# A decoder layer with routed experts: one expert instead of two loaded ahead of the route, and eight narrow tiles instead of seven

## The chip, the cores and the metric

One core of a Trainium2 chip runs the whole program. The metric is device time in microseconds (us) of one execution, lower is better; three executions of a kernel give its median. The engines are TensorE (PE in the rows), VectorE (DVE), ScalarE (ACT), GpSimd (POOL) and SyncE (SP). SP does nothing but ask for transfers; POOL asks for the gathers.

## The reference

One layer serves 512 prompt tokens and 64 sample tokens (576 in all, width 1024, all float32). After the mixing sub-layer (attention beside a spatial gate, then an output projection) comes a mixture of experts:

```python
h2 = rms_norm(x, g_pre_ffn) * (1 + sc2) + sh2
# hier_moe(h2): best of 4 groups, then top 2 of its 4 experts; 16 experts, weights from two softmaxes
for e in range(N_EXPERTS):
    hdn = jax.nn.silu(x @ w_gate[e]) * (x @ w_up[e])     # (N, 1024) @ (1024, 512), twice
    y = y + gates[:, e:e + 1] * (hdn @ w_down[e])        # (N, 512) @ (512, 1024)
x = x + ga2 * rms_norm(y, g_post_ffn)
```

Each token goes to two experts, so 1152 places are filled. `w_gate`, `w_up` and `w_down` of one expert are 2 MB each, 6 MB together, 96 MB for the sixteen.

## The kernel before

The program is one block after another: `condition`, `project`, `attend_prompt`, `attend_sample`, `merge`, `experts`, `later_tiles`, `combine`. Every engine has its own list of instructions, in the order of the code, and waits on semaphores.

**Tiles.** The tokens of an expert are gathered into a tile. `experts` handles MAIN = 16 tiles, one for each expert. A wide tile has 128 places, a narrow one 64 (`wide`, `places`, HALF). In a wide tile gate (line 2454) and up (line 2464) are two runs of eight 128x512 matmuls, and down (line 2489) is two more runs of four. In a narrow tile gate (line 2461) goes to one half of the output rows and up (line 2464) to the other, in turn, and down (line 2494) does the same with its two column halves. A matmul in float32 shows as two passes, so a run of eight has x16 in the trace. Lines 2426 and 2519 are the transposes of the gathered tokens and of h.

TensorE's order in tile e is: gate and up of e, the token transposes of e+1, down of e-1, the transposes of h of e. TILE_AT gives the number of the tile that is done at place e of the order; before it is 0, 1, 2, 4, 3, 6, 5, ..., 14, 13, 15. Tiles 0, 1, 2 and the even ones are wide (nine), the other seven narrow. The two tiles of the end (LAST) are narrow.

**Which expert is in which tile.** Experts 0 to FIXED-1 are always in tiles 0 to FIXED-1, whatever their number of tokens. The others are ranked by it at run time (`key`, `narrow`, `place` in VectorE's part of `merge`), the WIDE = 7 largest go to the wide tiles, the rest to the narrow ones. Tokens that do not fit go to overflow tiles of `later_tiles`, a loop that runs only if there are any.

**Loads.** Weights lie in a ring of eight slots of 2 MB; `expert_slot` gives slot and count for each (e, kind), kind being 0 for gate, 1 for up, 2 for down. Load q = 3e + kind needs the slot of load q-8, so SP waits for the end of gate, up or down of an earlier tile first. Those of fixed experts need no knowledge of the route. The loads of expert 0 are asked for at the end of `merge`, as soon as the sample group's attention has left its slots; so is gate of expert 1, behind them. Then come the five stores of h2 to memory (`store(t)`, line 1862), which the gathers read. Up and down of expert 1 are asked for once gather 0 has landed. Then SP waits for `order_done`, the semaphore that says which expert is in which tile, and from there on asks for tile after tile, with the store of the results of tile e-3 behind the loads of tile e.

**The h2 buffers.** The five tiles of h2 use two buffers in part: before h2 of tiles 2 and 3 is computed, VectorE waits until the store of tile 0 or 1 has landed:

```python
                if t in (2, 3):
                    dve.wait_ge(h2_out2[t % 2], 16)
```

Behind h2 of the last tiles come, on VectorE, the logits, the choice of experts and the ranks (`route`, `first`), all of it serial. Gather 0 needs `first_ready` and the stores of h2. VectorE makes the table of the other tiles after the first gate has been multiplied (`table`, line 2436), and then `order_done` (line 2093).

Of the kernel before, what the change touches and what calls it, by code (L numbers as in the profile page):

```python
# [23 lines left out]
P = 128  # L24
# [11 lines left out]
NE, DE = 16, 512  # L36
# [3 lines left out]
BIG = 1e37  # L40
UNIT = 4096
MAIN = NE
FIXED = 2
WIDE = 7
HALF = P // 2
OVER = 10
NTILE = MAIN + OVER
TILE_AT = [0, 1, 2] + [e + 1 if e % 2 else e - 1 for e in range(3, MAIN - 1)] + [MAIN - 1]
LAST = (MAIN - 3, MAIN - 1)
EARLY = 3  # L50
ZERO_ROW = 3 * P + HALF
# [8 lines left out]
def wide(e):  # L60


    return e < FIXED or e % 2 == 0


def rows(t):
# [4 lines left out]
def constant_table():  # L71

    p = np.arange(P)[:, None]
    cols = {}
    cols["ident"] = np.eye(P)
    x = np.arange(512)[None, :] - 384
    cols["dist"] = np.where(p - x >= 0, p - x, BIG)
    t, h = p % ST, p // 16
    slope = 2.0 ** -(h + 1.0)
    r = np.arange(120)[None, :] - 56  # L80
    cols["own"] = np.where((r >= 0) & (r <= t), -slope * (t - r), -BIG)
    cols["tril"] = (np.arange(P)[None, :] <= p) * 1.0
    c64 = np.arange(NS)[None, :]
    cols["sameseq"] = (c64 // ST == p // ST) * 1.0
    cols["repeat"] = (c64 % ST == p) * 1.0
    cols["before"] = (p < np.arange(P)[None, :]) * 1.0
    cols["ones"] = np.ones((P, P))
    e = np.arange(NE)
    cols["earlier"] = np.broadcast_to((e[None, :] < e[:, None]).reshape(1, -1), (P, NE * NE)) * 1.0
    cols["desc"] = np.broadcast_to([4.0, 3.0, 2.0, 1.0], (P, 4))  # L90
    cols["group"] = (p // 32 == np.arange(4)[None, :]) * 1.0
    cols["diag"] = ((p // ST) % 4 == np.arange(4)[None, :]) * 1.0
    row = (p // 16) * ST + t
    first = (p // ST) % 2 == 0
    cols["sel1"] = ((row == c64) & first) * 1.0
    cols["sel2"] = ((row == c64) & ~first) * 1.0
    cols["half"] = np.full((P, H), -0.5)
    cols["token"] = p + P * np.arange(NT)[None, :] * 1.0
    cols["row"] = np.broadcast_to(np.arange(P)[None, :] * 1.0, (P, P))
    cols["tilestart"] = np.broadcast_to(P * np.arange(NTILE + 1)[None, :] * 1.0, (P, NTILE + 1))  # L100
    cols["pagerow"] = p % PAGEROWS * 1.0
    tie = np.where(e < FIXED, 20000.0 - 1000.0 * e, NE - 1.0 - e)
    cols["tie"] = np.broadcast_to(tie[None, :], (P, NE))
    cols["place0"] = np.broadcast_to(np.where(e < FIXED, -128.0 * e, -256.0)[None, :], (P, NE))
    at, parts = {}, []
    n = 0
    for name, a in cols.items():
        a = np.broadcast_to(a, (P, a.shape[1]))
        at[name] = (n, a.shape[1])
        n += a.shape[1]  # L110
        parts.append(a)
    at["mainbase"] = at["tilestart"][0], NE
    at["index"] = at["row"][0], OVER

    past = -slope * (PAST + t - np.arange(PAST).reshape(2, P, ROWKEYS).transpose(0, 2, 1).reshape(1, PAST))
    return at, np.ascontiguousarray(np.concatenate(parts, 1).astype(np.float32)), \
        np.ascontiguousarray(past.astype(np.float32))
# [101 lines left out]
class Program:  # L219
# [614 lines left out]
    def attend_prompt(self, block):  # L834
# [3 lines left out]
        nc, a, o, L, PS = self.nc, self.a, self.o, self.L, self.PS  # L838
# [3 lines left out]
        dchain, pchain, zeroed = self.dve_chain, self.pool_chain, self.sem("c_zeroed")  # L842
# [38 lines left out]
        @block.gpsimd  # L881
        def _(pool):
            link = chain(pool, pchain, self.pool_count)

            pool.wait_ge(self.lam_sum, 1)
            pool.wait_ge(grp_done, 3 * NT)
            self.load_pages(pool, self.ck, 0, 0, K_SLOT[0][0])
            pool.wait_ge(self.ada_done, 3)
            self.load_pages(pool, self.ck, 0, 1, K_SLOT[0][1])
            self.load_pages(pool, self.cv, 0, 0, V_SLOT[0])  # L890

            link(pool.memset(L.mix[:, 4, 0:512], 0.0))
            unused = self.y_rows[FIXED * P:(LAST[0] + 1) * P].rearrange("(i q p) n -> p i q n", i=WIDE - 1, p=HALF)
            for c in range(2):
                cols = slice(512 * c, 512 * c + 512)
                pool.dma_start(unused[:, :, 3, cols], L.mix[0:HALF, 4:5, 0:512].to_broadcast([HALF, WIDE - 1, 512])
                               ).then_inc(zeroed, 16)
                pool.dma_start(unused[:, WIDE - 2, 2, cols], L.mix[0:HALF, 4, 0:512]).then_inc(zeroed, 16)
            for i in range(3):
                pool.wait_ge(ss_ready, i + 1)  # L900
                self.power(pool, link, ss, H, P, 1.0 / DV, ss_power)
            pool.wait_ge(grp_done, group_at("q", 4) + 1)
            self.load_pages(pool, self.ck, 1, 0, K_SLOT[1][0])
            pool.wait_ge(grp_done, group_at("v", 4) + 1)
            self.load_pages(pool, self.cv, 0, 1, V_SLOT[1])
            pool.memset(L.at(n1, 1280), 0.0).then_inc(self.blank, 1)
            pool.wait_ge(pv_done, N)
            self.load_pages(pool, self.ck, 1, 1, K_SLOT[1][1])
            pool.wait_ge(zeroed, 64)

            def last_power():
                pool.wait_ge(ss_ready, 4)
                self.power(pool, link, ss, H, P, 1.0 / DV, ss_power)
            self.last_power = last_power
# [862 lines left out]
    def merge(self, block):  # L1777
# [3 lines left out]
        nc, a, L, PS = self.nc, self.a, self.L, self.PS  # L1781
# [49 lines left out]
        key, narrow, place, filled = (take(n, NE) for n in ("key", "narrow", "place", "filled"))  # L1831
# [4 lines left out]
        n = r0 + 1024  # L1836
# [21 lines left out]
        def _(sp):  # L1858
# [17 lines left out]
                self.load_expert(sp, 0, 0, kind)  # L1876
            sp.wait_ge(self.sample["pv"], SB)
            self.load_expert(sp, 0, 0, 2)
            self.load_expert(sp, 1, 1, 0)
            for t in range(NT):  # L1880
                store(t)

# [31 lines left out]
        def _(dve):  # L1914
# [85 lines left out]
            for c in range(2):  # L2000
# [39 lines left out]
            dve.wait_ge(first_index, 1)  # L2040
            dve.tensor_copy(self.ints[:, 0:1], PS[:, 0, 0:1]).then_inc(self.first_ready, 1)
            link(dve.tensor_scalar(narrow, key, FIXED + WIDE - 0.5, None, ALU.is_ge))
            dve.scalar_tensor_tensor(place, narrow, float(P * (2 - FIXED - 2 * WIDE + 1)), L.cst("place0"),
                                     ALU.mult, ALU.add).then_inc(dchain, 1)
            link.count[0] += 1
            link(dve.tensor_scalar(narrow, narrow, float(HALF), None, ALU.mult))
# [152 lines left out]
    def experts(self, block):  # L2199
# [4 lines left out]
        nc, L, PS = self.nc, self.L, self.PS  # L2204
# [25 lines left out]
        def places(e):  # L2230


            return P if wide(TILE_AT[min(e, MAIN - 1)]) else HALF

# [12 lines left out]
        def _(sp):  # L2247
            def store(e):
                n = places(e)
                sp.wait_ge(y_a, self.up(y_a, e + 1))  # L2250
                sp.wait_ge(y_d, self.up(y_d, e + 1))
                sp.dma_start(self.y_rows[P * TILE_AT[e]:P * TILE_AT[e] + n], B["y"][e % 2][0:n]).then_inc(y_out[e % 2], 16)

            for i in range(2):
                sp.wait_ge(self.h2_outs[i], (48, 32)[i])
            sp.wait_ge(xg_in[0], self.up(xg_in[0], 16))
            self.load_expert(sp, 1, 1, 1)
            self.load_expert(sp, 1, 1, 2)
            sp.wait_ge(self.order_done, 1)
            for e in range(FIXED, MAIN):  # L2260
                own = sp.value_load(self.ints[0:1, 80 + TILE_AT[e]:81 + TILE_AT[e]], min_val=0, max_val=NE - 1)
                for kind in range(3):
                    q = 3 * e + kind - 8
# [536 lines left out]
```

## Time and profile before

| | before |
|---|---|
| three runs, us | 844.1, 839.42, 849.49 |
| median, us | 844.1 |
| the profiled execution, us | 844.71, of which 842.9 are its span |
| TensorE busy | 761.0 us, 90% of the span |
| VectorE, ScalarE, GpSimd busy | 361.7, 184.0, 116.5 us |
| bytes moved, mean rate | 249.5 MB, 296 GB/s |
| mean granted clock of TensorE | 0.948 of full |
| chain that ended last | 74% TensorE, 10% DMA, 9% VectorE |

The span is the time between the first and the last event of the profiled execution; all starts are counted from it. In the rows "x16" is a count, the number in brackets at the end of a row in order of time is how long the engine was idle before it and what released it. The experts' stage runs from gather 0 (516) to about 815 us, the combination of the results and the output take the rest.

### The profile page before, as it was taken

What the parts mean: (1) busy time and instruction counts of PE and PEld (TensorE: products, weight loads), DVE (VectorE), ACT (ScalarE), POOL (GpSimd) and SP (SyncE); (2) the same over time, 40 slices, a digit from 0 to 9 for tenths busy, and PEclk for the clock granted to TensorE, in tenths of its full rate; (3) what the DMA queues carried; (4) which work ended last, traced back from release to release, by engine and by line L of the source; (5) the groups of instructions that cost most, each with busy time, mean ns of one, the idle gap of its engine ahead of it and who ended that gap; (6) DMA issues with size and microseconds to landing.
All of it is one profiled execution on the core that took longest, in us unless ns stands there. A gap on an engine that the chain in (4) does not pass through costs nothing.

```text
span 842.9 us, 12264 instructions
## 1 busy us (share of the span) xinstructions
PE 761.0 (90%) x5020; PEld 366.9 (44%) x5020; DVE 361.7 (43%) x830; ACT 184.0 (22%) x426; POOL 116.5 (14%) x169
## 2 busy tenths in 40 slices
PE   4699999999999839999999744999999999999994
PEld 3244343444444524545555333544444444444431
DVE  2212252536798846947665667100131011010146
ACT  4001000124454412413333211011011011110132
POOL 2220000200001111313221200100000000000054
PEclk9899999999999969979899965999999999999997
DMA  8979096580000996999999944788899999999793
GB/s 305 400 229 416 30 393 215 159 300 14 13 2 20 368 403 272 422 384 353 415 376 349 389 194 160 301 342 331 313 408 407 421 397 398 422 386 402 310 310 113
DMA packets 36602, 249.52 MB, mean 296 GB/s; under 512 B 4137, under 2 KB 5417, under 8 KB 23106
## 3 DMA queue, kind: packets, MB, share of 16 engines
q1 hardware_dynamic: 26482, 165.02, 50.5%
q0 software_dynamic: 9120, 81.34, 24.7%
q10 hardware_dynamic: 944, 2.38, 0.7%
q8 instruction: 40, 0.66, 0.3%
q14 instruction: 16, 0.13, 0.0%
HBM read 232.32 MB, written 16.40 MB: 295 GB/s over the span
## 4 chain that ended last, share of the span: by engine, by line
PE 74%; DMA 10%; DVE 9%; issue 2%; POOL 2%; SPq 2%; ACT 1%; POOLq 0%; DVEq 0%; ACTq 0%
PE ps L778 10%; PE ps L2454 8%; PE ps L2464 7%; PE ps L2489 7%; PE ps L1679 6%; PE ps L1069 5%; PE ps L2461 5%; PE ps L1597 4%; DMA sb<-in_w_ada 3%; PE ps L1647 3%; PE ps L2494 2%; DMA sb<-in_w_out 2%; PE ps L2426 2%; PE ps L535 2%; PE ps L1625 2%
## 5 line engine op out<-in xcount | busy, mean ns | idle before, releaser
L2464 PE MATMUL ps<-sb 128*128 128x512 f32 (+1 forms) x256 | 112.9, 594 | 0.0
L778 PE MATMUL ps<-sb 128*128 128x512 f32 x192 | 87.4, 610 | 1.4 <-DVE sb L436 1.4
L2388 DVE TENSOR_TENSOR sb<-sb,ps 128x512 f32<-128x512 f32 (+1 forms) x16 | 10.9, 684 | 160.4 <-PE ps L2464 94.7
L817 DVE STREAM_TRANSPOSE sb<-sb 128x1024 f32<-128x1024 f32 (+1 forms) x72 | 76.5, 1099 | 0.0
L2454 PE MATMUL ps<-sb 128*128 128x512 f32 x144 | 65.5, 608 | 1.0 <-ACT sb L2306 0.9
L2489 PE MATMUL ps<-sb 128*128 128x512 f32 x144 | 63.5, 594 | 0.0
L1679 PE MATMUL ps<-sb 128*128 128x512 f32 x128 | 61.9, 640 | 0.0
L1069 PE MATMUL ps<-sb 128*128 128x512 f32 x128 | 59.2, 597 | 0.3 <-DVE sb L972 0.3
L2464 PEld LDWEIGHTS ps<-sb 128*128 128x128 f32 (+1 forms) x256 | 42.0, 167 | 34.0 <-issue 34.0
L778 PEld LDWEIGHTS ps<-sb 128*128 128x128 f32 x192 | 36.5, 195 | 46.0 <-issue 42.9
L2461 PE MATMUL ps<-sb 128*64 128x512 f32 x112 | 49.6, 595 | 0.0
L2283 POOL DMA_INDIRECT sb<-h_rows,ints x16 | 14.9, 933 | 242.2 <-PE ps L2426 209.6
L946 ACT ACTIVATE sb<-sb 128x128 f32<-128x128 f32 (+3 forms) x64 | 35.4, 554 | 53.6 <-DVE sb L1030 53.6
L2399 DVE COPY sb<-ps 128x512 f32<-128x512 f32 (+1 forms) x16 | 11.1, 692 | 73.9 <-PE ps L2489 56.2
L2454 PEld LDWEIGHTS ps<-sb 128*128 128x128 f32 x144 | 27.3, 195 | 32.9 <-issue 31.0
L1597 PE MATMUL ps<-sb 32*32 32x512 f32 x1024 | 38.3, 612 | 2.7 <-issue 2.6
L1030 DVE CUSTOM_DVE_ANT_0 sb<-ps,sb 128x128 f32<-128x128 f32 (+3 forms) x64 | 28.7, 486 | 26.6 <-PE ps L1104 26.5
L1679 PEld LDWEIGHTS ps<-sb 128*128 128x128 f32 x128 | 25.5, 205 | 33.3 <-issue 33.1
L2489 PEld LDWEIGHTS ps<-sb 128*128 128x128 f32 x144 | 26.7, 190 | 30.3 <-issue 30.1
L1069 PEld LDWEIGHTS ps<-sb 128*128 128x128 f32 x128 | 22.9, 193 | 22.1 <-issue 20.9
L2317 ACT ACTIVATE sb<-ps 128x512 f32<-128x512 f32 (+1 forms) x16 | 9.5, 596 | 105.3 <-PE ps L2454 60.2
L1647 PE MATMUL ps<-sb 128*32 128x256 f32 x512 | 29.3, 381 | 1.0 <-ACT sb L1405 1.0
(347 smaller groups left out, 993.5 us busy)
## 6 DMA issues: line engine op xcount, KB each, us to landing
sb<-in_w_gate SPq DMA_DIRECT2D x16, 2048.0 KB, 19.0
sb<-in_w_up SPq DMA_DIRECT2D x16, 2048.0 KB, 9.9
sb<-in_w_down SPq DMA_DIRECT2D x16, 2048.0 KB, 14.4
sb<-in_w_ada SPq DMA_DIRECT2D x12, 2048.0 KB, 18.6
sb<-in_w_in SPq DMA_DIRECT2D x5, 2048.0 KB, 27.8
y_rows<-sb SPq DMA_DIRECT2D x9, 512.0 KB, 16.0
sb<-in_x_prompt SPq DMA_DIRECT2D x8, 512.0 KB, 6.7
sb<-in_w_out SPq DMA_DIRECT2D x2, 2048.0 KB, 20.6
```

The lines of the kernel that those rows point to most:

```text
L778: last = pe.matmul(PS[:, n % 4, :], L.hT[:, k, t * P:t * P + P], w[:, k, :], start=k == 0, stop=k == KC - 1)
L817: dve.transpose(block, block).then_inc(self.turned, 1)
L946: act.activation(pb[n % 3][j][:, 0:w], pb[n % 3][j][:, 0:w], ACT.Exp, bias=nm[:, q:q + 1], scale=-1.0, accum_out=sums[:, q:q + 1]).then_in ...
L1030: dve.tensor_tensor_reduce(out=pb[n % 3][j][:, 0:w], in0=PS[:, 2 * (n % 2) + j, 0:w], in1=self.dist_bias[:, h, 384 - P * i:512], scale=-1. ...
L1069: last = pe.matmul(PS[:, bank, :], L.hT[:, k, t * P:t * P + P], w[:, k, :], start=k == 0, stop=k == KC - 1)
L1597: last = pe.matmul(PS[32 * h:32 * h + 32, g, :], qst[par][r, h, 32 * c:32 * c + 32], kp[r, :, at_row:at_row + 32], start=c == 0, stop=c == 3)
L1647: last = pe.matmul(PS[c:c + 32, 7, 0:256], at[:, page, 32 * quad:32 * quad + 32], vp[:, g, 256 * quad:256 * quad + 256], start=page < 2, s ...
L1679: last = pe.matmul(PS[:, 5, :], mixT(t)[:, k, :], wo[c][:, k, :], start=k == 0, stop=k == KC - 1)
L2454: last = pe.matmul(PS[:, 0, :], x[:, k, :], w_gate[:, k, :], start=k == 0, stop=k == KC - 1)
L2461: last = pe.matmul(PS[n:P, 0, :], x[:, k, :], w_gate[:, k, :], start=k == 0, stop=k == KC - 1)
L2464: last = pe.matmul(PS[0:n, 1, :], x[:, k, :], w_up[:, k, :], start=k == 0, stop=k == KC - 1)
L2489: last = pe.matmul(PS[:, 5 + c, :], hT[:, k, :], w[:, k, 512 * c:512 * c + 512], start=k == 0, stop=k == FC - 1)
```

## The change

FIXED goes from 2 to 1. Expert 1 is now ranked with the others; WIDE stays 7, so there are eight wide tiles (the even ones) and eight narrow ones, and the order of tiles becomes 0, 2, 1, 4, 3, ..., 14, 13, 15. The third place in the order is a narrow tile now. The numbers in the computation of `place` follow. The three loads of expert 1 ahead of `order_done` are gone: the second tile's weights are asked for in the loop, by the expert that the order names. The rows of narrow tiles that no store fills, zeroed at the start, grow by one half tile.

```diff
--- before.py
+++ after.py
@@ -40,12 +40,12 @@
 BIG = 1e37
 UNIT = 4096
 MAIN = NE
-FIXED = 2
+FIXED = 1
 WIDE = 7
 HALF = P // 2
 OVER = 10
 NTILE = MAIN + OVER
-TILE_AT = [0, 1, 2] + [e + 1 if e % 2 else e - 1 for e in range(3, MAIN - 1)] + [MAIN - 1]
+TILE_AT = [0] + [e + 1 if e % 2 else e - 1 for e in range(1, MAIN - 1)] + [MAIN - 1]
 LAST = (MAIN - 3, MAIN - 1)
 EARLY = 3
 ZERO_ROW = 3 * P + HALF
@@ -60,7 +60,7 @@
 def wide(e):
 
 
-    return e < FIXED or e % 2 == 0
+    return e % 2 == 0
 
 
 def rows(t):
@@ -101,7 +101,7 @@
     cols["pagerow"] = p % PAGEROWS * 1.0
     tie = np.where(e < FIXED, 20000.0 - 1000.0 * e, NE - 1.0 - e)
     cols["tie"] = np.broadcast_to(tie[None, :], (P, NE))
-    cols["place0"] = np.broadcast_to(np.where(e < FIXED, -128.0 * e, -256.0)[None, :], (P, NE))
+    cols["place0"] = np.broadcast_to(np.where(e < FIXED, -128.0 * e, 256.0 - 256.0 * FIXED)[None, :], (P, NE))
     at, parts = {}, []
     n = 0
     for name, a in cols.items():
@@ -890,12 +890,12 @@
             self.load_pages(pool, self.cv, 0, 0, V_SLOT[0])
 
             link(pool.memset(L.mix[:, 4, 0:512], 0.0))
-            unused = self.y_rows[FIXED * P:(LAST[0] + 1) * P].rearrange("(i q p) n -> p i q n", i=WIDE - 1, p=HALF)
+            unused = self.y_rows[0:(LAST[0] + 1) * P].rearrange("(i q p) n -> p i q n", i=WIDE, p=HALF)
             for c in range(2):
                 cols = slice(512 * c, 512 * c + 512)
-                pool.dma_start(unused[:, :, 3, cols], L.mix[0:HALF, 4:5, 0:512].to_broadcast([HALF, WIDE - 1, 512])
+                pool.dma_start(unused[:, :, 3, cols], L.mix[0:HALF, 4:5, 0:512].to_broadcast([HALF, WIDE, 512])
                                ).then_inc(zeroed, 16)
-                pool.dma_start(unused[:, WIDE - 2, 2, cols], L.mix[0:HALF, 4, 0:512]).then_inc(zeroed, 16)
+                pool.dma_start(unused[:, WIDE - 1, 2, cols], L.mix[0:HALF, 4, 0:512]).then_inc(zeroed, 16)
             for i in range(3):
                 pool.wait_ge(ss_ready, i + 1)
                 self.power(pool, link, ss, H, P, 1.0 / DV, ss_power)
@@ -1876,7 +1876,6 @@
                 self.load_expert(sp, 0, 0, kind)
             sp.wait_ge(self.sample["pv"], SB)
             self.load_expert(sp, 0, 0, 2)
-            self.load_expert(sp, 1, 1, 0)
             for t in range(NT):
                 store(t)
 
@@ -2040,7 +2039,7 @@
             dve.wait_ge(first_index, 1)
             dve.tensor_copy(self.ints[:, 0:1], PS[:, 0, 0:1]).then_inc(self.first_ready, 1)
             link(dve.tensor_scalar(narrow, key, FIXED + WIDE - 0.5, None, ALU.is_ge))
-            dve.scalar_tensor_tensor(place, narrow, float(P * (2 - FIXED - 2 * WIDE + 1)), L.cst("place0"),
+            dve.scalar_tensor_tensor(place, narrow, float(P * (1 - 2 * (FIXED + WIDE))), L.cst("place0"),
                                      ALU.mult, ALU.add).then_inc(dchain, 1)
             link.count[0] += 1
             link(dve.tensor_scalar(narrow, narrow, float(HALF), None, ALU.mult))
@@ -2254,8 +2253,6 @@
             for i in range(2):
                 sp.wait_ge(self.h2_outs[i], (48, 32)[i])
             sp.wait_ge(xg_in[0], self.up(xg_in[0], 16))
-            self.load_expert(sp, 1, 1, 1)
-            self.load_expert(sp, 1, 1, 2)
             sp.wait_ge(self.order_done, 1)
             for e in range(FIXED, MAIN):
                 own = sp.value_load(self.ints[0:1, 80 + TILE_AT[e]:81 + TILE_AT[e]], min_val=0, max_val=NE - 1)
```

SP, from the end of `merge` into `experts`: `L1773` are the loads of weights, `L1862` the stores of h2, and the first TENSOR_LOAD stands directly behind the wait for `order_done`. Before:

```order
L1773 DMA sb<-in_w_down 128x4096
L1773 DMA sb<-in_w_gate 128x4096
L1862 DMA h_rows<-sb 128x1024 x4
L1862 DMA h_rows<-sb 64x1024
L2246 UNCONDITIONAL_BRANCH
L1773 DMA sb<-in_w_up 128x4096
L1773 DMA sb<-in_w_down 128x4096
L2261 TENSOR_LOAD ints
L2261 ISA x2
L1773 ISA
L1773 DMA sb<-in_w_gate 128x4096
```

After:

```order
L1773 DMA sb<-in_w_down 128x4096
L1862 DMA h_rows<-sb 128x1024 x4
L1862 DMA h_rows<-sb 64x1024
L2245 UNCONDITIONAL_BRANCH
L2258 TENSOR_LOAD ints
L2258 ISA x2
L1773 ISA
L1773 DMA sb<-in_w_gate 128x4096
L1773 DMA sb<-in_w_up 128x4096
L1773 DMA sb<-in_w_down 128x4096
```

The gate load ahead of the stores and the up and down loads behind them have gone; the first load after the TENSOR_LOAD is that of the second tile (before, of the third), and the three loads that follow are the third's.

TensorE, second tile and the start of the third. In before, `L2454` and `L2464` are gate and up of the second tile, then token transposes of the third, down of the first, h transposes of the second, and gate and up of the third:

```order
L2454 MATMUL ps<-sb 128x512 x8
L2464 MATMUL ps<-sb 128x512 x8
L2426 MATMUL ps<-sb 128x128 x8
L2489 MATMUL ps<-sb 128x512 x8
L2519 MATMUL ps<-sb 128x128 x4
L2454 MATMUL ps<-sb 128x512 x8
L2464 MATMUL ps<-sb 128x512 x8
L2426 MATMUL ps<-sb 128x128 x8
L2489 MATMUL ps<-sb 128x512 x8
L2519 MATMUL ps<-sb 128x128 x4
```

After, where lines 2451, 2461, 2423, 2486, 2516 stand for 2454, 2464, 2426, 2489, 2519 and line 2458 for 2461:

```order
L2451 MATMUL ps<-sb 128x512 x8
L2461 MATMUL ps<-sb 128x512 x8
L2423 MATMUL ps<-sb 128x64 x8
L2486 MATMUL ps<-sb 128x512 x8
L2516 MATMUL ps<-sb 128x128 x4
L2458 MATMUL ps<-sb 64x512
L2461 MATMUL ps<-sb 64x512
L2458 MATMUL ps<-sb 64x512
```

The third tile's tokens are transposed at 64 places, and its gate and up alternate in pairs on 64 rows (eight pairs, two shown), where before they were two runs on 128.

## Rows read from the trace of the kernel before

**Rows 1.** Busy by stretches, 480 to 520: us, engines, granted clock, DMA share, GB/s
```profile
480.00:500.00 20.00, 10.42 (x69) 6.38 (x69) 13.58 (x16) 4.68 (x12) 4.39 (x6) 0.72 0.72 303
500.00:520.00 20.00, 7.01 (x40) 6.44 (x40) 15.38 (x60) 1.38 (x5) 1.75 (x3) 0.50 0.20 66
```

**Rows 2.** Busy by stretches, the experts' stage
```profile
537.00:615.00 78.00, 77.89 (x230) 36.65 (x230) 12.45 (x41) 7.82 (x14) 3.71 (x4) 1.00 0.87 339
620.00:780.00 160.00, 160.00 (x539) 70.28 (x539) 18.04 (x31) 19.28 (x36) 7.36 (x8) 1.00 1.00 405
```

**Rows 3.** SP's queue in order of time: start, us, line, transfer
```profile
474.12 0.33 SPq L1773 DMA_DIRECT2D sb<-in_w_down  x1
474.89 0.34 SPq L1773 DMA_DIRECT2D sb<-in_w_gate  x1
483.97 23.20 SPq L1862 DMA_DIRECT2D h_rows<-sb  x5
...
536.80 0.35 SPq L1773 DMA_DIRECT2D sb<-in_w_gate  x1
...
541.36 0.34 SPq L1773 DMA_DIRECT2D sb<-in_w_gate  x1
...
783.27 0.33 SPq L1773 DMA_DIRECT2D sb<-in_w_up  x1
```

**Rows 4.** Transfers asked for at 474.12, 474.89, 483.97: size, us to landing
```profile
sb<-in_w_down SPq DMA_DIRECT2D x1, 2048.0 KB, 13.8
...
sb<-in_w_gate SPq DMA_DIRECT2D x1, 2048.0 KB, 17.9
...
h_rows<-sb SPq DMA_DIRECT2D x1, 512.0 KB, 10.1
```

**Rows 5.** VectorE in order of time, with idle time before and its releaser
```profile
494.20 1.28 DVE L1924 SCALAR_TENSOR_TENSOR sb<-sb 128x1024 f32<-128x1024 f32 x1 [4.91 <-DMA h_rows<-sb]
...
499.22 0.24 DVE L1931 SCALAR_TENSOR_TENSOR sb<-sb 128x20 f32<-128x20 f32 x1
```

**Rows 6.** The chain of waits between 481 and 496
```profile
483.97 10.14 DMA h_rows<-sb
```

**Rows 7.** ScalarE in order of time, the copy of the logits
```profile
494.11 0.19 ACT L1372 ACTIVATE sb<-ps 128x20 f32<-128x20 f32 x1 [2.71 <-PE ps L1706]
```

**Rows 8.** Transfers asked for at 536.80, 537.25, 541.36: size, us to landing
```profile
sb<-in_w_gate SPq DMA_DIRECT2D x1, 2048.0 KB, 11.3
...
sb<-in_w_up SPq DMA_DIRECT2D x1, 2048.0 KB, 17.0
...
sb<-in_w_gate SPq DMA_DIRECT2D x1, 2048.0 KB, 24.3
```

**Rows 9.** The chain of waits in the experts' stage: start, us, engine, line
```profile
564.61 0.47 PE ps L2519 x4
565.08 6.87 PE ps L2454 x16
...
586.57 0.47 PE ps L2519 x4
...
694.44 0.62 PE ps L2519 x4
...
729.25 0.62 PE ps L2519 x4
```

**Rows 10.** TensorE in order of time, tokens and gate of the first tile, gate of the second
```profile
520.36 1.97 PE L2426 MATMUL ps<-sb 128*128 128x128 f32 x8 [4.77 <-DMA sb<-h_rows,ints]
523.23 8.65 PE L2454 MATMUL ps<-sb 128*128 128x512 f32 x16 [0.90 <-ACT sb L2306]
...
542.89 7.11 PE L2454 MATMUL ps<-sb 128*128 128x512 f32 x16
```

**Rows 11.** The transfer asked for at 783.27: size, us to landing
```profile
sb<-in_w_up SPq DMA_DIRECT2D x1, 2048.0 KB, 8.1
```

**Rows 12.** TensorE in order of time, first gate matmul of the last tile
```profile
799.56 0.64 PE L2461 MATMUL ps<-sb 128*64 128x512 f32 x1
```

## The prediction

> **What bounds the kernel now.** I read first the busy time by stretches, then the chain of waits around the route, then the engines in order of time, then the landing of single transfers. In [rows 1] the reader is to see that from 480 to 520 TensorE is busy only 10.4 and 7.0 of 20 us: this is the tail of the mixing sub-layer and the route, a chain on VectorE. In [rows 2] it is busy for all of the 160 us from 620 to 780, at a granted clock of 1.00: the experts are bound by TensorE. But there the DMA engines are at a share of 1.00 as well. The two resources are nearly even, and the change takes work from the one and gives work to the other.
>
> **Part 1: the order ahead of the route.** The load of `w_gate` of expert 1 is asked for at 474.89, ahead of the stores of `h2` on the same queue [rows 3]. [rows 4] show what that costs: it takes 17.9 us to land (492.8), and the first store, asked for at 483.97, lands 10.1 later (494.1), 1.3 behind it. VectorE waits for that store, 4.91 us before 494.20 [rows 5], since h2 of the third token tile overwrites the buffer that the store reads; and the chain of waits runs through it [rows 6]. Without the load, the store stands behind `w_down` of expert 0, asked for at 474.12, which lands 13.8 later, at 487.9 [rows 3, 4]; half a megabyte behind a load took 1.3, so it lands at 489.2, and VectorE is free for it at 489.3 (494.20 - 4.91). What is late next? ScalarE's copy of the logits ends at 494.30 [rows 7]. VectorE comes to the step that needs it at 499.22 [rows 5], and would now at 494.3. So nearly the whole wait goes: **-4.8 us** for all that follows, gather 0 and `order_done` among it. Ends: 0 (something not seen is late) and -4.9.
>
> **Part 2: three loads that now follow the route.** Gate, up and down of the second tile leave their two places ahead of `order_done` on SP's queue and come first behind it. That wait ended at 536.80 [rows 3], now at 536.8 - 4.8 = 532.0. The first load behind it took 11.3 us to land [rows 8], since gathers of two tiles go ahead of it. The gather of the third tile is half as long now, so I take 11.0, and the load lands at 543.0. TensorE wants it at 542.89 [rows 10] less 4.8, that is 538.1. **+4.9 us** of waiting; ends 4.0 and 5.5. The second load lands 17.0 behind its issue half a microsecond later [rows 8], at 549.5, and is wanted 7.1 behind 543.0, at 550.1: no wait, with little to spare. Parts 1 and 2 cancel: what the earlier route gives, the later weights take.
>
> The wait has a second price. After a gap TensorE's granted clock goes to the lower of its levels (1.2 of 2.4 GHz) for a while; in [rows 1] the stretch 500 to 520 is at 0.50 throughout. [rows 10] show the cost: sixteen passes of one gate matrix take 8.65 us behind the gap ahead of gather 0's matmuls, and 7.11 behind none. A gap of 4.9 us is as long as the one there (4.77, in the row at 520.36). I take **+1.5**, with 0 and +3.0 (the lower level lasts twice as long) as ends.
> The Trainium skill ("TensorE: Matmul & The Clock Gate", Part 1: The HAM clock gate) says that the lower clock is the default, that activity lifts it, and that the time until it does varies from run to run. By that rule the term is somewhere between those ends and not nought; the trace agrees in that the clock is down after each of its long gaps.
>
> **Part 3: one tile of 128 places becomes one of 64.** It is the third in order. A step of a 128 behind a 128, from one transpose of h to the next, is 586.57 - 564.61 = 21.96 us; a pair of a 128 and a 64 is 729.25 - 694.44 = 34.81 [rows 9]. So the 64 costs 12.85, and the exchange gives **-9.1 us** of TensorE time, all of it on the engine that bounds the stage; ends -8.8 and -9.3, for other switches between the shapes. The instructions of the route are as many as before; only numbers in them change. The rows zeroed at the start grow by 256 KB, 0.65 us of transfer at 405 GB/s; I cost them at nothing, since nobody waits for them before the last gathers: the projections, hundreds of us earlier, hide them. Without that cover they would cost their 0.65.
>
> Whether eight experts fit in 64 places is a matter of data. From the reference's inputs I count 66 tokens for expert 0; of the others the eight smallest have 59, 50, 48, 48, 47, 38, 36 and 30. So there is no overflow tile, before or after.
>
> **Part 4: can the weights keep up?** From `order_done` to the landing of the last `w_up`, SP's and POOL's queues now carry 44 loads of 2.1 MB (92.3 MB), 5.8 MB of gathered rows and 5.0 MB of stored results: 103.3 MB with instruction fetches. Before it was 41 loads and 97.3 MB in all. I take the rate of a full queue from the 160 us in [rows 2], 405 GB/s. The 78 us before it moved at 339, so 78 x (1 - 339/405) = 12.7 us of them were empty. Put to the test on before: 537.6 + 97,300/405 + 12.7 = 790.5, and the last `w_up` landed at 783.27 + 8.1 = 791.4 [rows 3, 11]. Now the queue has no empty stretch: 532.8 + 103,300/405 = 787.9, say 789. TensorE wanted it at 799.56 [rows 12], and now at 799.56 + 0.1 + 1.5 - 9.1 = 792.1. Some 3 us are left: no wait, term **0**. The early part is as close. The third tile needs gate and up at once, at 565.1 + 1.5 = 566.6 (565.08 is where the third tile began, [rows 9]). Its `w_up` is the fifth load; before, the fourth landed at 541.36 + 24.3 = 565.7 [rows 3, 8], 28.9 behind the first issue. With 5 more for a load and 1.9 less for the gathers that are not yet there or half as long: 532.0 + 32 = 564. In time.
> The Trainium skill ("DMA: Bandwidth & Descriptors", Specifications) puts the limit of one core to and from HBM at about 358 GB/s. By that figure 103.3 MB would take 289 us and the last `w_up` would land near 821, as an estimate 29 us late, and the change would lose some 20. [rows 2] disagree, 405 over 160 us, and the sum goes by them.
>
> **The sum.** -4.8 + 4.9 + 1.5 - 9.1 + 0 = -7.5 us. The profiled execution took 844.7 us (span 842.9), so that gives 837.2; the median of the three runs, 844.1, is 0.6 lower: **836.6 us**. The runs lie 10 us apart, so 1% (8.4 us) is about what a measurement of this kernel can tell from no change, and the gain that I forecast is just under it.
>
> **The rivals.**
> A, the wait is cheap: the clock stays up, and the first load lands within 10 us. -4.8 + 3.9 - 9.1 = -10.0: **834.1**. For: TensorE is full for some 20 us ahead of the gap. Against: the clock is down behind the gaps that the trace has.
> B, the DMA queue becomes the bound. The tiles of 64 wait for `w_up` when a full queue moves less than 103,300/(792.1 - 532.8) = 398 GB/s. At 395 the price is 2 us, at 390 it is 5.6: **839 to 842**. For: the last `w_up` landed only 799.56 - 791.4 = 8.2 us ahead of its use [rows 11, 12], and part 3 moves that use 7.5 forward. Against: the mean of 160 us.
> C, the store was not what held the route, so that of the 4.8 us 1 comes, while the late weights cost their 4.9 in full: **840.4**. This is the case in which the new order does not give what it seems to. For: several threads join there. Against: [rows 7].
> D, slower than before: the mechanism of B below 103,300/(799.6 - 532.8) = 387 GB/s, because loads, gathers and stores now overlap without a pause from `order_done` on. At 380 the last `w_up` lands at 804.6, 5 later than its use before: **849**. Against: a rate 6% under what the same mixture of transfers reached.
>
> **How the numbers follow.** My sum 0.46, A 0.18, B 0.18, C 0.12, D 0.06. The range reaches down to 829 (A, with -9.3 for the tile, and the spread of the runs) and up to 844 (B and C with theirs); outside are D and the tails. Faster by over 1%, under 835.7: A, and somewhat under half of my own case, 0.38. Slower by over 1%: 0.05, D. Within 1%: 0.57.
>
> **What the changed kernel's profile would show.** VectorE's wait for the store of h2 at most 0.5 us, and gather 0 at 511.3 in place of 516.1. A new wait of TensorE of about 5 us at 538, for `w_gate` of the second tile, and slower matmuls behind it. The third tile without a wait, the DMA share at 1.0 from 537 on, the last gate and up at 792. I am wrong if TensorE waits ahead of the tiles of 64 (B, D), if gather 0 is no earlier (C), or if rows of the looped block for overflow tiles appear.

## The result, and the profile after

Over 17 executions of each the changed kernel takes 835.45 us (median, 830.02 to 839.04), the kernel before 842.98 (838.23 to 849.49). The ratio is 0.9911, 95% interval 0.9892 to 0.9929: 7.5 us faster, between 6.0 and 9.1. The profiled execution took 837.01 us.

I read the pair of profiles as four stretches, cut at events that both have. The head ends where VectorE begins the first step that reads the last rows loaded for `merge` (471.98 before, 470.05 after). The route goes from there to TensorE's token transposes of tile 0. The experts' stage goes on to the end of the last down; the tail is the rest of the span.

| us | before | after | difference |
|---|---|---|---|
| head | 471.98 | 470.05 | -1.93 |
| route | 48.38 | 44.31 | -4.07 |
| experts' stage | 294.90 | 291.92 | -2.98 |
| tail | 27.64 | 28.92 | +1.28 |
| span | 842.9 | 835.2 | -7.7 |

The head is not the change's: over the ten profiles of this study, of kernels that differ behind it or in one small transfer inside it, it ended between 463.06 and 473.46, with no order to it. So a single pair of spans says less than its stretches do.

The page's first lines, after:

```profile
span 835.2 us, 12272 instructions
...
PE 750.8 (90%) x5020; PEld 358.6 (43%) x5020; DVE 361.2 (43%) x830; ACT 183.8 (22%) x426; POOL 117.3 (14%) x169
```

TensorE's busy time fell from 761.0 to 750.8, and its share stayed at 90%.

**The route.** VectorE in order of time, after; a bracket is the idle time before a row and who ended it. To be held against [rows 5]:

```profile
487.28 1.27 DVE L1923 SCALAR_TENSOR_TENSOR sb<-sb 128x1024 f32<-128x1024 f32 x1
...
490.58 1.28 DVE L2007 SCALAR_TENSOR_TENSOR sb<-ps,sb 64x1024 f32<-64x1024 f32 x1 [0.78 <-POOL sb L832]
...
493.14 0.24 DVE L1930 SCALAR_TENSOR_TENSOR sb<-sb 128x20 f32<-128x20 f32 x1
```

The row at 487.28 is the step that stood 4.91 us for the store of h2; it has no bracket now. The store itself (the only one asked for at 482.04), size and time to landing, beside the 10.1 of [rows 4]:

```profile
h_rows<-sb SPq DMA_DIRECT2D x1, 512.0 KB, 4.9
```

But 0.78 us of waiting have come up two steps on, for GpSimd's root of the norm. GpSimd in order of time:

```profile
488.59 1.26 POOL L831 TENSOR_SCALAR sb<-sb 64x1 f32<-64x1 f32 x1 [6.17 <-ACT sb L1339]
489.93 0.54 POOL L832 TENSOR_TENSOR sb<-sb 64x1 f32<-64x1 f32 x1
494.38 0.18 POOL L831 TENSOR_SCALAR sb<-sb 64x1 f32<-64x1 f32 x1 [3.90 <-ACT sb L1339]
```

Line 831 on 64x1 takes 1.26 us here and 0.18 at 494.38. At 488.59 VectorE is at work on h2 (487.28 to 489.80); before, it stood idle beside the same root. So 4.91 - 0.78, and 4.07 in the stretch.

**The second tile.** SP's queue, after, against [rows 3]: `order_done` has come 5.7 us earlier on the clock of the profile, and the first load behind it is the second tile's.

```profile
531.07 0.36 SPq L1773 DMA_DIRECT2D sb<-in_w_gate  x1
531.53 0.38 SPq L1773 DMA_DIRECT2D sb<-in_w_up  x1
...
533.60 1.40 SPq L1773 DMA_DIRECT2D sb<-in_w_up  x1
```

Landing of these three, gate and up of the second tile and up of the third:

```profile
sb<-in_w_gate SPq DMA_DIRECT2D x1, 2048.0 KB, 9.8
...
sb<-in_w_up SPq DMA_DIRECT2D x1, 2048.0 KB, 15.4
...
sb<-in_w_up SPq DMA_DIRECT2D x1, 2048.0 KB, 28.7
```

Gate is there at 531.07 + 9.8 = 540.9, up of the third tile, the fifth load, at 533.60 + 28.7 = 562.3. TensorE:

```profile
514.36 1.97 PE L2423 MATMUL ps<-sb 128*128 128x128 f32 x8 [4.83 <-DMA sb<-h_rows,ints]
517.23 8.84 PE L2451 MATMUL ps<-sb 128*128 128x512 f32 x16 [0.90 <-ACT sb L2303]
...
536.22 0.75 PE L2516 MATMUL ps<-sb 128*128 128x128 f32 x4
540.97 8.80 PE L2451 MATMUL ps<-sb 128*128 128x512 f32 x16 [4.00 <-DMA sb<-in_w_gate]
549.61 7.03 PE L2461 MATMUL ps<-sb 128*128 128x512 f32 x16
```

The h transposes of tile 0 end at 536.97. Then comes the new wait, 4.00 us for `w_gate`, and behind it gate's sixteen passes take 8.80 in place of the 7.11 of [rows 10]. The granted clock tells why (columns as in [rows 1]):

```profile
540.00:541.00 1.00, 0.03 (x1) 0.06 (x1) 0.00 (x0) 0.00 (x0) 0.00 (x0) 1.00 0.91 389
541.00:542.00 1.00, 1.00 (x2) 0.50 (x3) 0.00 (x0) 0.00 (x0) 0.00 (x0) 0.60 1.00 410
542.00:543.00 1.00, 1.00 (x2) 0.42 (x2) 0.00 (x0) 0.00 (x0) 0.00 (x0) 0.50 1.08 446
...
545.00:546.00 1.00, 1.00 (x4) 0.46 (x3) 0.00 (x0) 0.00 (x0) 0.00 (x0) 1.00 1.15 483
```

It is at its upper level while TensorE is idle, falls in the row of 541, after work has begun again at 540.97, stands at the lower level, 1.2 GHz, in the row of 542, and is back up by 545.

**The tile of 64, and the weights.** The chain of waits, at the h transposes of the second, third and fourth tile, against [rows 9]:

```profile
564.73 0.47 PE ps L2516 x4
...
580.17 0.62 PE ps L2516 x4
...
599.33 0.68 PE ps L2516 x4
```

The fourth tile's row in the chain of the kernel before:

```profile
608.87 0.47 PE ps L2519 x4
```

The step that ends at 586.57 before, 21.96 us after its start, now takes 580.17 - 564.73 = 15.44, which is 6.5 less. The next one, which holds the down of that tile, takes 599.33 - 580.17 = 19.16 in place of 608.87 - 586.57 = 22.30, another 3.1 less. The step behind that is 0.2 longer than before (16.09 against 15.88), so the exchange is worth 9.4 between these rows. The queue of transfers is full from the first load on, at the rate that it had before ([rows 2]):

```profile
533.00:615.00 82.00, 78.00 (x258) 35.18 (x256) 13.99 (x45) 8.80 (x16) 4.66 (x5) 0.98 1.00 408
615.00:775.00 160.00, 160.00 (x549) 70.14 (x550) 18.84 (x32) 20.31 (x38) 7.36 (x8) 1.00 1.01 407
```

The last `w_up`, asked for at 773.94, and TensorE's first use of it:

```profile
sb<-in_w_up SPq DMA_DIRECT2D x1, 2048.0 KB, 12.3
```
```profile
790.24 0.64 PE L2458 MATMUL ps<-sb 128*64 128x512 f32 x1
```

It lands at 786.2, 4.0 us ahead of 790.24. TensorE waits for no weights but the second tile's gate.

### The profile page after: what moved, and what is told of

The parts are those of the page before. It is cut to its first block, busy times and chain, and to the rows that moved or that the text cites. A ratio compares the mean times of both kernels' runs of the same rounds, so it can differ in the third digit from the quotient of the medians.

```text
span 835.2 us, 12272 instructions
## 1 busy us (share of the span) xinstructions
PE 750.8 (90%) x5020; PEld 358.6 (43%) x5020; DVE 361.2 (43%) x830; ACT 183.8 (22%) x426; POOL 117.3 (14%) x169
## 4 chain that ended last, share of the span: by engine, by line
PE 72%; DVE 10%; DMA 10%; issue 2%; SPq 2%; POOL 2%; ACT 1%; another core or an unknown queue 1%; POOLq 0%; DVEq 0%; ACTq 0%
PE ps L778 10%; PE ps L2451 7%; PE ps L2486 7%; PE ps L1679 6%; PE ps L2461 6%; PE ps L2458 6%; PE ps L1069 5%; PE ps L1597 4%; DMA sb<-in_w_ada 3%; PE ps L1647 3%; PE ps L2491 3%; PE ps L535 2%; DMA sb<-in_w_out 2%; PE ps L2423 2%; DMA sb<-in_x_sample 2%
## 5 line engine op out<-in xcount | busy, mean ns | idle before, releaser
L778 PE MATMUL ps<-sb 128*128 128x512 f32 x192 | 87.8, 612 | 1.4 <-DVE sb L436 1.4
L2451 PE MATMUL ps<-sb 128*128 128x512 f32 x128 | 60.4, 627 | 4.9 <-DMA sb<-in_w_gate 4.0
L1069 PE MATMUL ps<-sb 128*128 128x512 f32 x128 | 59.2, 597 | 0.3 <-DVE sb L972 0.3
L1679 PE MATMUL ps<-sb 128*128 128x512 f32 x128 | 58.8, 614 | 0.0
L2458 PE MATMUL ps<-sb 128*64 128x512 f32 x128 | 56.6, 595 | 0.0
L778 PEld LDWEIGHTS ps<-sb 128*128 128x128 f32 x192 | 36.7, 196 | 46.2 <-issue 44.9
L2486 PE MATMUL ps<-sb 128*128 128x512 f32 x128 | 56.5, 594 | 0.0
L2451 PEld LDWEIGHTS ps<-sb 128*128 128x128 f32 x128 | 24.9, 200 | 34.8 <-issue 33.1
L1679 PEld LDWEIGHTS ps<-sb 128*128 128x128 f32 x128 | 24.2, 194 | 31.6 <-issue 31.4
L2486 PEld LDWEIGHTS ps<-sb 128*128 128x128 f32 x128 | 23.7, 190 | 26.9 <-issue 26.8
L1069 PEld LDWEIGHTS ps<-sb 128*128 128x128 f32 x128 | 22.9, 193 | 22.0 <-issue 20.9
```

Source lines behind the costliest of these rows:

```text
L778: last = pe.matmul(PS[:, n % 4, :], L.hT[:, k, t * P:t * P + P], w[:, k, :], start=k == 0, stop=k == KC - 1)
L1069: last = pe.matmul(PS[:, bank, :], L.hT[:, k, t * P:t * P + P], w[:, k, :], start=k == 0, stop=k == KC - 1)
L1679: last = pe.matmul(PS[:, 5, :], mixT(t)[:, k, :], wo[c][:, k, :], start=k == 0, stop=k == KC - 1)
L2451: last = pe.matmul(PS[:, 0, :], x[:, k, :], w_gate[:, k, :], start=k == 0, stop=k == KC - 1)
L2458: last = pe.matmul(PS[n:P, 0, :], x[:, k, :], w_gate[:, k, :], start=k == 0, stop=k == KC - 1)
L2486: last = pe.matmul(PS[:, 5 + c, :], hT[:, k, :], w[:, k, 512 * c:512 * c + 512], start=k == 0, stop=k == FC - 1)
```

## The experiments

Each ran five rounds against the kernel before on the same chip; stretches are those of the table above, from its profile.

| kernel | ratio to before (95%) | route | stage | tail |
|---|---|---|---|---|
| changed | 0.9911 (0.9892 to 0.9929) | 44.31 | 291.92 | 28.92 |
| e1_gate_behind_stores | 0.9965 (0.9932 to 0.9997) | 44.34 | 296.68 | 28.54 |
| e2_loads_behind_order | 0.9981 (0.9951 to 1.0011) | 44.14 | 297.63 | 27.57 |
| e3_narrow_alone | 0.9881 (0.9838 to 0.9924) | 48.10 | 286.82 | 27.64 |
| e4_order_before_table | 0.9932 (0.9905 to 0.9959) | 44.28 | 293.36 | 28.82 |
| e5_filler_in_the_gap | 0.9900 (0.9866 to 0.9934) | 44.86 | 291.83 | 28.75 |
| e6_early_order_gather_first | 0.9835 (0.9804 to 0.9866) | 44.25 | 289.73 | 27.58 |
| e7_narrow_and_gate_behind_stores | 0.9849 (0.9813 to 0.9884) | 44.18 | 286.73 | 27.63 |
| e8_order_earlier_still | 0.9810 (0.9761 to 0.9858) | 44.23 | 286.35 | 27.60 |

**e1_gate_behind_stores**: part 1 alone.

```diff
-            self.load_expert(sp, 1, 1, 0)
             for t in range(NT):
                 store(t)
+            self.load_expert(sp, 1, 1, 0)
```

> The kernel before, with one load moved: gate of expert 1 is asked for behind the five stores of h2 and not ahead of them. Nothing else changes. Theory (the store of h2 stood behind that load and held the route): VectorE's wait for the store goes from 4.9 to 0 us, something small takes its place (0.8 on GpSimd's root, as in the changed kernel), gather 0 comes 4.1 earlier, no wait for weights arises since gate of expert 1 has 50 us to land: 4.1 us faster than before, ratio 0.995. Rival (the route is held by another thread, the store only ended last): gather 0 no earlier than 1 us, ratio 0.999 to 1.000.

The route is 4.04 us shorter. The wait for the store is gone, and VectorE's next one is, as expected:

```profile
489.28 1.28 DVE L2008 SCALAR_TENSOR_TENSOR sb<-ps,sb 64x1024 f32<-64x1024 f32 x1 [0.78 <-POOL sb L832]
```

By time it is 2.9 us faster, interval 0.3 to 5.7: the theory's 4.1 lies inside, and only the upper end touches the rival's 0.999 to 1.000. In the trace the rest went to three places that have nothing to do with the store: gate of tile 0 took 9.64 us in place of 8.65, since the lower clock lasted longer (it was back up some 5.1 us after gate's start in place of 3.1), the wait ahead of the last down was 1.70 in place of 0.91, and the tail is 0.9 longer. So the load held the store, and the store held the route.

**e2_loads_behind_order**: parts 1 and 2, without the narrow tile.

```diff
-            self.load_expert(sp, 1, 1, 0)
             for t in range(NT):
                 store(t)
...
-            self.load_expert(sp, 1, 1, 1)
-            self.load_expert(sp, 1, 1, 2)
             sp.wait_ge(self.order_done, 1)
+            for kind in range(3):
+                self.load_expert(sp, 1, 1, kind)
```

> The kernel before, with the three loads of expert 1 asked for right behind the wait for order_done; its tile stays at 128 places. It is the order half of the change alone. Theory: -4.1 (route earlier), +4.0 (TensorE waits for gate of the second tile), +1.7 (gate at the lower clock): 1.6 us slower than before, ratio 1.002; later tiles without a wait. Rival (with the wide tile kept the queue has slack, but three more loads behind the route leave the weights late again and again): further waits of TensorE for weights, 3 to 8 us, ratio 1.005 to 1.01.

```profile
517.60 1.97 PE L2425 MATMUL ps<-sb 128*128 128x128 f32 x8 [4.67 <-DMA sb<-h_rows,ints]
520.47 9.38 PE L2453 MATMUL ps<-sb 128*128 128x512 f32 x16 [0.90 <-ACT sb L2305]
...
543.25 7.11 PE L2453 MATMUL ps<-sb 128*128 128x512 f32 x16 [2.49 <-DMA sb<-in_w_gate]
```

The wait is 2.49 us here, not 4.00, and gate behind it runs at the full 7.11. Gate of tile 0, which took 9.38, made TensorE later, and the load landed in 9.2 us. The time, 1.6 us faster with an interval that holds no change, misses the 1.6 slower that I expected; the interval ends just short of it. There is no other wait for weights, though 45 loads now follow the route, so the rival falls as well. What stands: the earlier route and the later weights about cancel, but the price of a wait of some us is not a constant. It was 2.5 in this profile, 5.7 in the changed kernel's.

**e3_narrow_alone**: part 3 without parts 1 and 2. The second tile is narrow and still expert 1's, whose 48 tokens fit; its loads stand where they stood.

```diff
-    return e < FIXED or e % 2 == 0
+    return e % 2 == 0
...
             link(dve.tensor_scalar(narrow, narrow, float(HALF), None, ALU.mult))
+            link(dve.memset(narrow[:, 1:2], float(HALF)))
```

(The zeroed rows are those of the change.)

> The kernel before, loads in the order of before, but tile 1 has 64 places and stays expert 1's (48 tokens in the reference's inputs); the second tile in the order is narrow. It is the tile half of the change alone. Theory (TensorE bounds the stage, the queue keeps up): 9.1 us faster, ratio 0.989, VectorE's wait for the store of h2 still 4.9. Rival (the queue of weights is the bound from 620 on, since its share is 1.0 there): the 9.1 come back as waits for w_up of narrow tiles; 3 to 5 us faster, ratio 0.995.

```profile
490.06 1.28 DVE L1924 SCALAR_TENSOR_TENSOR sb<-sb 128x1024 f32<-128x1024 f32 x1 [4.61 <-DMA h_rows<-sb]
```
```profile
516.24 1.97 PE L2427 MATMUL ps<-sb 128*128 128x128 f32 x8 [4.78 <-DMA sb<-h_rows,ints]
519.11 10.10 PE L2455 MATMUL ps<-sb 128*128 128x512 f32 x16 [0.90 <-ACT sb L2307]
```

VectorE still waits 4.61 us for the store, and the route is 48.10. The stage is 8.08 shorter although gate of tile 0 took 10.10, 1.45 more than before. Without that it would be 9.5 shorter: 0.3 of this is a shorter wait ahead of the last down (0.62 against 0.91), and 9.2 is left for the tile. By time it is 10.0 faster, interval 6.4 to 13.7. The forecast 9.1 holds and the rival's 0.995 lies outside. The full queue did not take any of it back.

**e4_order_before_table**: the changed kernel with the four steps that lead to `order_done` ahead of VectorE's wait for the table.

```diff
+            link(dve.tensor_tensor(oa, place.unsqueeze(1).to_broadcast([P, NE, NE]),
+                                   L.cst("mainbase").unsqueeze(2).to_broadcast([P, NE, NE]), ALU.is_equal))
...
+            dve.tensor_copy(self.ints[:, 80:80 + NE], key).then_inc(self.order_done, 1)
             dve.wait_ge(self.table_made, 1)
             dve.tensor_copy(self.ints[:, 1:NTILE], PS[:, 6, 1:NTILE]).then_inc(table_done, 1)
-            link(dve.tensor_tensor(oa, place.unsqueeze(1).to_broadcast([P, NE, NE]),
...
-            dve.tensor_copy(self.ints[:, 80:80 + NE], key).then_inc(self.order_done, 1)
```

> The changed kernel, with the four steps on VectorE that name the expert of each tile (and signal order_done) moved ahead of its wait for the table of places; VectorE is idle 7.4 us there. order_done comes 7.5 us earlier, near 523.6. Theory: gate of the second tile lands near 533, before TensorE wants it at 537; the wait of 4.0 and the slow clock of 1.7 both go: 5.7 us faster than the changed kernel, ratio to before 0.984 to 0.985. Rival (the first loads then stand behind gathers or one another, and the wait moves to w_up of the third tile): 2 to 3 us faster than the changed kernel, ratio 0.988.

Both expectations failed. Gate of the second tile now lands at 523.07 + 7.5 = 530.6, long before its use, and yet the kernel is no faster than the changed one. Landing of that gate, and of gather 1, the tokens of the second tile:

```profile
sb<-in_w_gate SPq DMA_DIRECT2D x1, 2048.0 KB, 7.5
...
sb<-h_rows,ints POOLq DMA_INDIRECT x1, 10.8
```

TensorE:

```profile
539.62 1.97 PE L2423 MATMUL ps<-sb 128*128 128x128 f32 x8 [4.31 <-DMA sb<-h_rows,ints]
...
542.42 8.31 PE L2451 MATMUL ps<-sb 128*128 128x512 f32 x16
```

The wait is as long as before, 4.31, but for the tokens: gather 1 takes 10.8 us where it took 4.7 in the changed kernel and 4.1 in before, since six loads, 12 MB, had been asked for ahead of it (the next kernels vary just this number). Gate runs behind the gap at the lower clock again. The wait had not gone but changed its object.

**e5_filler_in_the_gap**: the changed kernel with work for TensorE in its gap.

```diff
+                if e == 1:
+                    for k in range(4):
+                        pe.matmul(PS[:, 7, :], L.cst("ones"), L.cst("dist"), start=k == 0, stop=k == 3)
                 if here:
                     gate_up(e, par, n)
```

> The changed kernel, with four matmuls of 128x512 on constants (eight passes, into a bank that nobody reads) ahead of the second tile's gate, so that TensorE works for 3.5 of the 4.0 us in which it waits for that gate's weights. Their result is not used. Theory (the second price of the wait is the clock, not slow weights): the wait shrinks to about 0.5 us, the granted clock stays at 1.00, and gate's sixteen passes take 7.1 in place of 8.8: 1.7 us faster than the changed kernel, ratio to before 0.989. Rival (gate is slow because its weights trickle in, or since transfers disturb it): 8.8 stays.

```profile
531.22 3.60 PE L2501 MATMUL ps<-sb 128*128 128x512 f32 x8
535.13 7.11 PE L2451 MATMUL ps<-sb 128*128 128x512 f32 x16 [0.31 <-DMA sb<-in_w_gate]
...
558.52 0.61 PE L2458 MATMUL ps<-sb 128*64 128x512 f32 x1 [0.86 <-DMA sb<-in_w_up]
```

The wait is 0.31, gate takes 7.11, the clock stays at 1.00: what the wait cost on top of itself was the clock, and the rival falls. But 0.86 of the gain was lost at once, in a wait of the third tile for its `w_up`, the fifth load, which in the changed kernel had landed 2.8 us ahead of its use (562.3 against 565.13). That is rival B's place, and it shows how little stood in hand there. Gate of tile 0 took another 0.85 us more than in the changed kernel (9.69 against 8.84), so the stage as a whole is only 0.09 shorter. The route is 0.55 longer: in this profile VectorE waited 0.72 us for the store of h2 again, which took 6.0 us to land. Against the changed kernel (0.9911) the time does not tell 0.9900 apart; that the cost was the clock rests on the rows of the trace.

**e6_early_order_gather_first**: e4, but only gate and up of the second tile are asked for ahead of gather 1.

```diff
                         sp.wait_ge(done, self.up(done, q // 3 + 1))
+                    if (e, kind) == (1, 2):
+                        sp.wait_ge(xg_in[1], self.up(xg_in[1], 16))
                     self.load_expert(sp, own, e, kind)
```

> The early order of e4_order_before_table, but SP asks only for gate and up of the second tile at once, and for the rest when gather 1 has landed. Theory (in e4 gather 1 took 10.9 us instead of 5 because four more loads, 8 MB, were in flight beside it): gather 1 lands by 535, gate by 531, up by 537, no wait of TensorE for either, the clock stays up: 5.5 us faster than the changed kernel, ratio to before 0.984 to 0.985. Rival (the gather is slow beside any load, also beside one): a wait of 2 to 4 us for gather 1 stays, with the slow clock behind it; ratio 0.989 to 0.991.

Gather 1, and TensorE:

```profile
sb<-h_rows,ints POOLq DMA_INDIRECT x1, 8.6
```
```profile
538.36 1.53 PE L2425 MATMUL ps<-sb 128*128 128x128 f32 x8 [2.08 <-DMA sb<-h_rows,ints]
...
540.73 7.93 PE L2453 MATMUL ps<-sb 128*128 128x512 f32 x16
```

The gather takes 8.6 us beside two loads, and 2.08 of the wait are left. The mechanism went between theory and rival; the time, 0.9835, met the theory's number. The profile accounts for part of it only: against the changed kernel's the stage is 2.19 us shorter and the tail 1.34, together 3.5 of the 6.4 us that lie between the two ratios. The time is clear of the changed kernel: the intervals do not touch.

**e7_narrow_and_gate_behind_stores**: e3 and e1 together.

```diff
-    return e < FIXED or e % 2 == 0
+    return e % 2 == 0
...
-            self.load_expert(sp, 1, 1, 0)
             for t in range(NT):
                 store(t)
+            self.load_expert(sp, 1, 1, 0)
...
+            link(dve.memset(narrow[:, 1:2], float(HALF)))
```

> e3_narrow_alone with the move of e1_gate_behind_stores: the second tile is narrow and stays expert 1's, gate of expert 1 is asked for behind the stores of h2, up and down behind gather 0. Theory (the two terms add, since the route and the stage are one behind the other): -9.1 and -4.1, so 13 us faster than before, ratio 0.984 to 0.985, with no wait for weights. Rival (they do not add: the faster stage is then held by the queue): 10 to 11 us, ratio 0.987 to 0.988, and waits of TensorE for weights of narrow tiles.

Route 44.18, stage 286.73, no wait for weights. Against before that is 4.20 less for the route and 8.17 less for the stage; e1 had 4.04 for the one and e3 8.08 for the other, so the two terms add. By time it is 12.7 us faster (9.8 to 15.8), near the theory's 13, but the interval also holds the rival's 0.987 to 0.988; it is the stretches and the missing waits that speak against the rival.

**e8_order_earlier_still**: e6 with the four steps further up.

```diff
             self.expert_evac_x(dve, 0, 0, P)
+            link(dve.tensor_tensor(oa, place.unsqueeze(1).to_broadcast([P, NE, NE]),
+                                   L.cst("mainbase").unsqueeze(2).to_broadcast([P, NE, NE]), ALU.is_equal))
...
+            dve.tensor_copy(self.ints[:, 80:80 + NE], key).then_inc(self.order_done, 1)
             sl = self.slotf.rearrange("p t j -> p (t j)")
```

> e6_early_order_gather_first, with the steps that name the experts moved further up on VectorE, behind its half of the first tile's transposes; the selection matrices behind them end 1.5 us later and are still there when TensorE comes to the table. order_done comes some 4.5 us earlier again (519.5 in the time of e6). Theory (gather 1 is slow in proportion to the loads in flight beside it): gate lands near 527 and up near 532, so gather 1, asked for at 529.7, shares the engines with 2 us of load and lands by 535.5; the wait of 2.1 us and the 0.8 of slow clock go: 2.9 us faster than e6, ratio to before 0.980. Rival (gather 1 takes its 8 us whatever is beside it, or the table comes later by what VectorE does first): the wait of 2 us stays, ratio 0.983 to 0.984.

Gate of the second tile, gather 1, and TensorE:

```profile
sb<-in_w_gate SPq DMA_DIRECT2D x1, 2048.0 KB, 7.6
...
sb<-h_rows,ints POOLq DMA_INDIRECT x1, 6.5
```
```profile
534.36 1.16 PE L2425 MATMUL ps<-sb 128*128 128x128 f32 x8
...
536.35 7.11 PE L2453 MATMUL ps<-sb 128*128 128x512 f32 x16 [0.35 <-ACT sb L2305]
```

The gather, asked for at 527.78, takes 6.5 us, since the second of the two loads lands 3.3 us after that (at 531.1), and TensorE comes to its tokens without a wait. The clock stays up. The stage is 286.35, 5.57 shorter than the changed kernel's, against the 5.7 that its wait and clock had cost. At 0.981, some 16 us faster than before and 8 faster than the changed kernel, this has the lowest ratio of those that were run, though the time does not tell it apart from e6 or e7. Unlike e3 and e7, it does not need expert 1 to fit in 64 places.

## Why the prediction was right

The forecast was 836.6, the measured median 835.45; the forecast difference -7.5, the measured -7.5. Term by term it is less even.

- **Part 1, the route, -4.8:** -4.07 in the pair, -4.04 in e1, -4.24 in e2. The mechanism was right and shown by e1 and e3. The size was too large by 0.7, because the step "what is late next" looked at ScalarE's logits and not at GpSimd's root, which takes 1.26 in place of 0.18 when VectorE works beside it.
- **Part 2, the wait, +4.9:** 4.00. The first load landed in 9.8 us, not 11.0. I carried 11.3 over from the kernel before and put it down to the two gathers of 128 places ahead of that load. The runs do not bear this reason out: in e2 the same two gathers went ahead and the load landed in 9.2. Over the seven profiles in which `order_done` comes behind the table it took between 8.7 (e7) and 11.4 (e1), and what sets it stays open. The clock, +1.5: 1.69, shown by e5 to be the clock. The assumption that a gap of this length must bring it down is not shown: behind 2.49 us in e2 it stayed up, behind 2.08 in e6 it fell (7.93).
- **Part 3, the tile, -9.1:** -2.98 = 4.00 + 1.69 + 0.19 (gate of tile 0, 8.84 against 8.65) + 0.34 (the wait ahead of the last down, 1.25 against 0.91) - 9.2, where 9.2 is what is left for the tile; the rows at the h transposes give 9.4. e3 has 9.2 alone.
- **Part 4, the queue, 0:** no wait. The rate was 407 and 408 GB/s against the assumed 405, the last `w_up` 4.0 us early against 3.1, the fifth load at 562.3 against 564. The Trainium skill's 358 GB/s ("DMA: Bandwidth & Descriptors", Specifications) does not bind here: by the prediction's estimate from it the change would have lost some 20 us.
- **Not in the sum:** the tail, +1.28. It comes in two lengths, 27.6 (before, e2, e3, e6, e7, e8) and 28.5 to 28.9 (changed, e1, e4, e5). In the changed kernel's long one VectorE copies the last down's second half late:

```profile
808.41 0.69 DVE L2396 COPY sb<-ps 64x512 f32<-64x512 f32 x1 [4.12 <-remote]
```

Down had ended at 806.28, and the releaser is none of the program's engines. ScalarE copies its half from 808.40, just as late. The length follows neither the loads nor the tile. It does go with GpSimd: in the four profiles with the long tail the last of its ten gathers of results had been issued within 0.3 us of the end of that down (806.26 in the changed kernel), in the six with the short one 1.35 to 1.82 us behind it. Whether that is a cause is not shown; nothing was tried on it.

The errors of the four terms, +0.7, -0.9, +0.2 and -0.1, cancel. What the sum lacked, +0.2, +0.3 and +1.3, makes the changed stretches of this pair of profiles 5.8 us shorter, not 7.5; the other 1.9 of its 7.7 are the head's. The 17 executions say 6.0 to 9.1. So the exact hit owes something to luck; how often the long tail comes in them is not known.

Of rival A (cheap wait) one half came: the load landed within 10 us, which made the wait 4.0. The other, that the clock stays up, did not, though it did in e2. B did not come: the fifth load landed 2.8 us ahead of its use, and in e5, without the gap's price, 0.9 us of such a wait appeared. C is refuted by e1's stretches, D by the rates.

## What to carry to other kernels

Look at what stands ahead of a store on the same queue, and at who waits for the store: here one load of 2 MB made it land 5.2 us later (10.1 against 4.9), as long as such a load takes at 405 GB/s. A load moved behind a late decision costs its wait, and the clock can come on top: it was at its lower level behind three of the four gaps of 2 us and more in which TensorE waited in this stage (changed, e4, e6), and not behind the fourth (e2). An earlier decision cures it, but few transfers may be asked for ahead of the next small gather that TensorE needs: with six ahead of it the same wait came back under another name, and it went only when two had nearly landed. Where an engine and the transfers are both full, work out the landing times of single loads against their use; here the landing of the last load came out within 1 us of the forecast margin (4.0 against 3.1).

## What the runs showed of the hardware

- An indirect gather of 128 rows of 4 KB took 4.1 us where no load had been asked for ahead of it (before), 6.5 where the last of two loads of 2 MB landed 3.3 us after the gather was asked for (e8), 8.6 behind two loads asked for 5.7 and 5.2 us earlier (e6), 10.8 behind six (e4).
- Three transfers on one queue landed one behind the other (487.9, 492.8 and 494.1 in before), and a store of 0.5 MB took 10.1 us behind two loads in flight. Behind one, which landed at 485.6 in the changed kernel, it took 4.9 and landed 1.3 after it.
- GpSimd's 64x1 step (line 831): 0.18 us while VectorE stood idle, 1.26 beside its work on h2, and 0.82 beside it in e5.
- TensorE's granted clock fell 0.2 us (changed) and 0.6 us (e6) after work had begun again behind gaps of 4.0 and 2.1 us, inside the gap of 4.3 us in e4, and not at all behind the gap of 2.5 us in e2. Gate of tile 0 took between 8.65 and 10.10 us in ten profiles of the same instructions behind a gap of 4.7 to 4.9 us.
